# Expert outputs kept as rows in DRAM and fetched per token, in place of scatter products, in a two-layer hybrid decoder step

## The chip, the cores and the metric

The program runs on one core of one Trainium2 chip. The metric is the time of one execution on the device, in microseconds (us). The kernel before was timed three times: 1644.41, 1648.15 and 1650.19 us, median 1648.15 us. One further execution was profiled, and all durations below come from its trace.

## The reference

The program computes two layers of a decoder trunk for 320 tokens: a prompt of 256 and 8 samples of 8. Each layer has a mixer (window attention, a short convolution and memory attention, gated and summed) and a channel part, each followed by a layer norm. The channel part of layer 0 is one dense SwiGLU network; that of layer 1 is a mixture of 8 experts, of which each token uses two. The change is in and around the mixture:

```python
def _moe(x, w_router, b_router, wg, wu, wd):
    xt = x.reshape(-1, D_MODEL)                                  # 320 x 1024
    logits = jnp.dot(xt, w_router, ...) + b_router
    top_v, top_i = lax.top_k(logits, TOP_K)                      # 2 of 8
    top_w = jax.nn.softmax(top_v, axis=-1)
    gates = jnp.sum(one_hot(top_i, N_EXPERTS) * top_w[..., None], axis=1)
    y = jnp.zeros_like(xt)
    for e in range(N_EXPERTS):
        y = y + gates[:, e:e + 1] * _swiglu(xt, wg[e], wu[e], wd[e])   # D_FF = 2816
    return y.reshape(shp)

x <- LayerNorm(ALPHA * x + ffn(x))
```

## The kernel before, in words

All weights are float32 and pass through the core once. The stream is cut into units of 1 MiB (128 partitions x 2048 numbers). SyncE (SP) loads a unit into a slot of `raw`; ScalarE (ACT) copies it, rounded, to `high` (`hi_moe`, L775; L768 in the dense part); VectorE (DVE) subtracts the two and leaves the remainder in `low` (`lo_moe`, L1063; L1072); TensorE (PE) then makes three products per tile, high weight by high activation, low by high, high by low. The dense part has six slots of `raw`, the mixture eleven, and `high` has three everywhere. So SP may load unit n when PE has finished unit n-11 (n-6 in the dense part), and ACT may copy unit n when PE has finished unit n-3. Each engine runs its own list in the order in which it is written, and semaphores (`unit_done`, `hi_done`, `lo_done`) tie the lists together.

After the second mixer the router picks two experts per token. Every expert has 128 slots, and `one_hot` (DVE) marks which token goes to which slot. The experts are worked in pairs: `pair_of_experts` on every engine goes through 66 units, 33 for each of two experts (j = 0 and j = 1; n counts units of one expert). Four pairs are run here: the first, a loop body that runs `loops` times, and two more; more rounds would be run if an expert had over 128 tokens. At the end of a pair PE gathers the tokens of the next pair with one-hot products (`gather`, L1868 to L1870, after units 28 to 31 of j = 1). Each expert has a down projection into PSUM banks 0 and 1; when its last unit is done, ACT copies it, scaled by the gate of each slot, to `ygh` (L1017) and DVE leaves the remainder in `ygl` (L1464).

Around the change, in the kernel before:

- `slots_of` (L1876, PE, after units 6 and 7 of j = 0) transposes the one-hot marks into `slot`, which DVE copies out (L1448); `gates_of` (L1883, PE, after unit 8) takes the gate of each slot by small products. Both are done in every pair.
- `scatter` (L1891, L1892, PE) multiplies `slot` by `ygh` and `ygl`, which puts an expert's rows back to their tokens. The six groups of the pair before are done one after each of units 0 to 5 of the next pair, four products each, and DVE adds each to `acc` (`add_back`, L1429). The last pair's groups are done after its last unit.
- `gate_columns` (DVE, L1379 to L1383) splits the gates of the pair for `gates_of`; it ends DVE's part of the router, before the first `lo_moe` of the mixture.

POOL (GpSimd) makes masks, issues the DMAs of caches and small outputs in both mixers, and is idle after the router. The layer norm at the end works on `acc`.

Of the kernel before, what the change touches and what calls it, by code (L numbers as in the profile page):

```python
# [28 lines left out]
ALU = mybir.AluOpType  # L29
# [106 lines left out]
SCATTER_AFTER = {n: n for n in range(6)}  # L136
SLOTS_AFTER = {6: 0, 7: 1}
GATES_AFTER = 8
SCATTER_BANK = (7, 0, 1, 7, 0, 1)
# [83 lines left out]
def build_trunk(nc, A, O):  # L223
    with ExitStack() as ctx:
# [20 lines left out]
        def sem(name):  # L245
# [84 lines left out]
        place["at"] = scratch_at  # L330
        xtokh = take("xtokh", [P, 2, D], F32R)
# [6 lines left out]
        sil = take("sil", [P, 2, 512])  # L338
        ygh = take("ygh", [P, 2, D], F32R)
# [29 lines left out]
        place["at"] = moe_end  # L369
        xeh = at("xeh", [P, KD, 2 * P], F32R, x_at)  # L370
# [8 lines left out]
                         for s in range(RING, RING_MOE)]  # L379
        gain = at("gain", [P, D], F32, ring_at + 4 * UNIT)  # L380
# [83 lines left out]
        scat_mm = sem("scat_mm")  # L464
        scat_cp = sem("scat_cp")
# [11 lines left out]
        y_lo = sem("y_lo")  # L477
        fin_mm = sem("fin_mm")
# [89 lines left out]
        def _(sp):  # L568
# [54 lines left out]
            sp.wait_ge(dma_mid, 16 * (8 + 20 * 2))  # L623
            pair_of_experts(0, first=True)
# [20 lines left out]
        def _(pool):  # L645
# [57 lines left out]
            for l in range(2):  # L703
# [35 lines left out]
                pool.wait_ge(dma_mid, 16 * (8 + 20 * (l + 1)))  # L739

# [6 lines left out]
            pool.memset(ygl[:, :, :].bitcast(F32), 0.0).then_inc(y_lo, 1)  # L747
# [5 lines left out]
            pool.wait_ge(dma_out, 16 * 4)  # L753
        CONSTS = 7
# [4 lines left out]
        def _(act):  # L759
# [290 lines left out]
        def _(dve):  # L1050
# [326 lines left out]
            def gate_columns(step):  # L1377

                dve.tensor_copy(gcur[:, :, :], gates[:, :, bass.ds(step * 2, 2)]).then_inc(gcur_done, 1)  # L1379
                dve.wait_ge(gcur_done, step + 1)  # L1380
                dve.tensor_copy(gsplit[:, :, :, 0], gcur[:, :, :]).then_inc(gc_hi, 1)
                dve.wait_ge(gc_hi, step + 1)
# [33 lines left out]
            gate_columns(0)  # L1416
# [7 lines left out]

            def add_back(count, g):

                half = slice(512 * (g % 2), 512 * (g % 2) + 512)
                dve.wait_ge(scat_mm, count + (g + 1))
                dve.tensor_tensor(acc[:, g // 2, half], acc[:, g // 2, half], ps[:, SCATTER_BANK[g], :],  # L1429
                                  ALU.add).then_inc(scat_cp, 1)  # L1430

            dve.wait_ge(acc_cp, 6)
            def pair_of_experts(step, before=0, first=False, final=False):
                for m in range(NPAIR):
# [8 lines left out]
                    if j == 0 and not first and n - 1 in SCATTER_AFTER:  # L1443
                        add_back(before * 6, SCATTER_AFTER[n - 1])
                    if j == 0 and n - 1 in SLOTS_AFTER:
                        i = SLOTS_AFTER[n - 1]
                        dve.wait_ge(slot_mm, step * 3 + (i + 1))
                        dve.tensor_copy(slot[:, i, 0:T], ps[:, SLOT_BANK[i], 0:T]).then_inc(slot_cp, 1)  # L1448
                    if j == 0 and n - 1 == GATES_AFTER:
                        dve.wait_ge(slot_mm, step * 3 + 3)  # L1450
# [6 lines left out]
                    if j == 1 and not final and n == ONE_HOT_AT:  # L1457
                        one_hot(step + 1)
                        gate_columns(step + 1)
                    if j == 1 and not final and n - 1 in GATHER_AFTER:  # L1460
                        tokens_lo(step * 4 + 4, GATHER_AFTER[n - 1], GATHER_BANK[GATHER_AFTER[n - 1]])
                    if n == NX - 1:
                        dve.wait_ge(y_hi, step * 2 + (j + 1))
# [49 lines left out]
        def _(pe):  # L1513
# [387 lines left out]
            def pair_of_experts(step, before=0, first=False, final=False):  # L1901
                for m in range(NPAIR):
# [5 lines left out]
                    if unit[0] == "d":  # L1908
# [3 lines left out]
                        if i == 0:  # L1912
                            pe.wait_ge(y_lo, step * 2 + (j + 1))
# [25 lines left out]
                    if n in TURN_AFTER:  # L1939
# [3 lines left out]
                        if j == 0 and h == 1:  # L1943
                            pe.wait_ge(slot_cp, step * 3 + 2)
# [3 lines left out]
                    if j == 0 and not first and n in SCATTER_AFTER:  # L1948
# [80 lines left out]
```

## Time and profile before

| | |
|---|---|
| three runs | 1644.41, 1648.15, 1650.19 us; median 1648.15 us |
| the profiled execution | 1647.17 us |
| its span, first to last instruction | 1645.4 us |
| mean granted TensorE clock | 0.989 |
| PE busy in the span | 1594.8 us (97%) |
| DVE busy | 1123.1 us (68%) |
| ACT busy | 918.6 us (56%) |
| POOL busy | 62.1 us (4%) |
| DMA, mean over the span | 239 GB/s |

Busy times are of one execution and overlap each other. The end of a matmul is modelled, so matmuls of one row of work overlap in the table; the distance from one start to the next tells what a matmul costs. "Idle" of an engine stands with what ended it. The mixture begins at about 829 us of the span and its last product is at about 1632 us.

### The profile page before, as it was taken

How to read it: one execution, taken by the hardware profiler on the slowest of the kernel's cores; microseconds unless marked ns; L12 is line 12 of the kernel's file. 1: busy time of each engine (PE TensorE's matmuls, PEld its weight loads, DVE VectorE, ACT ScalarE, POOL GpSimd, SP SyncE). 2: the span in 40 equal slices, each digit the busy share in tenths (PEclk: the TensorE clock that was granted, in tenths of full speed). 3: DMA queues.
4: the chain of work that ended last, by engine and by line, in shares of the span. 5: the costliest groups of instructions: out<-in, count | busy, mean ns of one | idle time of the engine just before them, and what ended most of it. 6: DMA issues, size and time to landing. Idle time of an engine off the chain costs nothing.

```text
span 1645.4 us, 22946 instructions
## 1 busy us (share of the span) xinstructions
PE 1594.8 (97%) x9167; PEld 1407.3 (86%) x9167; DVE 1123.1 (68%) x1031; ACT 918.6 (56%) x938; POOL 62.1 (4%) x114
## 2 busy tenths in 40 slices
PE   7999999899999899999799999999999999999996
PEld 6999899799999789989588888888888888888885
DVE  5545546644434535566488898888888888888887
ACT  4544443433322544444477776677766777667775
POOL 4103000000000002000100000000000000000000
PEclk9999999999999999999999999999999999999999
DMA  9746344244444244342679999899998999989981
GB/s 300 251 132 197 103 128 141 91 154 152 146 142 150 77 141 148 127 108 98 231 252 363 369 366 319 299 368 365 367 322 296 369 367 362 319 306 366 365 325 58
DMA packets 213033, 392.51 MB, mean 239 GB/s; under 512 B 8000, under 2 KB 98512, under 8 KB 212896
## 3 DMA queue, kind: packets, MB, share of 16 engines
q1 hardware_dynamic: 207520, 376.99, 66.8%
q0 software_dynamic: 5408, 14.06, 2.7%
q8 instruction: 74, 1.21, 0.3%
q14 instruction: 31, 0.25, 0.1%
HBM read 388.22 MB, written 4.76 MB: 239 GB/s over the span
## 4 chain that ended last, share of the span: by engine, by line
PE 94%; DVE 3%; ACT 1%; DMA 1%; issue 1%; SPq 0%; ACTq 0%; DVEq 0%
PE ps L1516 12%; PE ps L1518 12%; PE ps L1517 12%; PE ps L1935 10%; PE ps L1937 10%; PE ps L1936 10%; PE ps L1919 5%; PE ps L1921 5%; PE ps L1920 5%; PE ps L1946 1%; PE ps L1665 1%; DMA raw<-in_w_mem_k_dram 1%; PE ps L1771 1%; PE ps L1765 1%; PE ps L1639 1%; PE ps L1891 1%
## 5 line engine op out<-in xcount | busy, mean ns | idle before, releaser
L1063 DVE TENSOR_TENSOR low<-raw,high 128x2048 fp32r<-128x2048 f32 x264 | 604.0, 2291 | 104.5 <-ACT high L775 103.9
L775 ACT ACTIVATE high<-raw 128x2048 fp32r<-128x2048 f32 x264 | 505.8, 1918 | 234.1 <-PE ps L1937 142.8
L1516 PE MATMUL ps<-xh,high 128*128 128x320 f32 x1088 | 343.3, 316 | 9.7 <-DVE xl L1247 9.4
L1072 DVE TENSOR_TENSOR low<-raw,high 128x2048 fp32r<-128x2048 f32 x90 | 205.8, 2291 | 214.4 <-ACT high L768 214.3
L1517 PE MATMUL ps<-xh,low 128*128 128x320 f32 x1088 | 338.9, 311 | 0.0
L1518 PE MATMUL ps<-xl,high 128*128 128x320 f32 x1088 | 338.6, 311 | 0.0
L1935 PE MATMUL ps<-high,xeh 128*128 128x512 f32 (+1 forms) x768 | 291.8, 380 | 1.0 <-ACT row_f L999 1.0
L1937 PE MATMUL ps<-high,xel 128*128 128x512 f32 (+1 forms) x768 | 288.1, 375 | 0.0
L1936 PE MATMUL ps<-low,xeh 128*128 128x512 f32 (+1 forms) x768 | 287.8, 375 | 0.0
L768 ACT ACTIVATE high<-raw 128x2048 fp32r<-128x2048 f32 x90 | 171.9, 1910 | 169.8 <-PE ps L1518 156.5
L1516 PEld LDWEIGHTS ps<-xh,high 128*128 128x128 f32 x1088 | 207.5, 191 | 19.4 <-issue 18.5
L1517 PEld LDWEIGHTS ps<-xh,low 128*128 128x128 f32 x1088 | 207.5, 191 | 0.0
L1518 PEld LDWEIGHTS ps<-xl,high 128*128 128x128 f32 x1088 | 207.2, 190 | 0.0
L1935 PEld LDWEIGHTS ps<-high,xeh 128*128 128x128 f32 x768 | 144.2, 188 | 29.7 <-DVE low L1063 1.3
L1937 PEld LDWEIGHTS ps<-high,xel 128*128 128x128 f32 x768 | 144.3, 188 | 28.8
L1936 PEld LDWEIGHTS ps<-low,xeh 128*128 128x128 f32 x768 | 144.3, 188 | 26.9
L1919 PE MATMUL ps<-high,heh 128*128 128x512 f32 x352 | 141.2, 401 | 0.0
L1921 PE MATMUL ps<-high,hel 128*128 128x512 f32 x352 | 139.2, 395 | 0.0
L1920 PE MATMUL ps<-low,heh 128*128 128x512 f32 x352 | 138.6, 394 | 0.0
L1921 PEld LDWEIGHTS ps<-high,hel 128*128 128x128 f32 x352 | 66.0, 188 | 16.3
L1920 PEld LDWEIGHTS ps<-low,heh 128*128 128x128 f32 x352 | 66.2, 188 | 14.6
L1919 PEld LDWEIGHTS ps<-high,heh 128*128 128x128 f32 x352 | 66.1, 188 | 14.5
(323 smaller groups left out, 1680.8 us busy)
## 6 DMA issues: line engine op xcount, KB each, us to landing
raw<-in_exp_w_gate_dram SPq DMA_DIRECT2D x88, 1024.0 KB, 5.3
raw<-in_exp_w_up_dram SPq DMA_DIRECT2D x88, 1024.0 KB, 5.4
raw<-in_exp_w_down_dram SPq DMA_DIRECT2D x88, 1024.0 KB, 5.3
raw<-in_w_in_dram SPq DMA_DIRECT2D x37, 1024.0 KB, 5.3
raw<-in_ffn_w_gate_dram SPq DMA_DIRECT2D x11, 1024.0 KB, 5.4
raw<-in_ffn_w_up_dram SPq DMA_DIRECT2D x11, 1024.0 KB, 5.3
raw<-in_ffn_w_down_dram SPq DMA_DIRECT2D x11, 1024.0 KB, 4.9
raw<-in_w_o_dram SPq DMA_DIRECT2D x8, 1024.0 KB, 5.2
```

Source lines behind the costliest of these rows:

```text
L775: act.activation(high[(N_DENSE + m) % HI_RING][:, :], raw_moe[s][:, :], ACT.Copy).then_inc(hi_done, 1)
L1063: dve.tensor_tensor(low_moe[s][:, :], raw_moe[s][:, :], high[(N_DENSE + m) % HI_RING][:, :].bitcast(F32), ALU.subtract).then_inc(lo_done, 1)
L1072: dve.tensor_tensor(low[n % RING][:, :], raw[n % RING][:, :], high[n % HI_RING][:, :].bitcast(F32), ALU.subtract).then_inc(lo_done, 1)
L1516: pe.matmul(out, wh, ah, start=first, stop=False)
L1517: pe.matmul(out, wl, ah, start=False, stop=False)
L1518: return pe.matmul(out, wh, al, start=False, stop=last)
L1919: pe.matmul(out, heh[:, tile, :], wh[:, c], start=i == 0 and k == 0, stop=False)
L1920: pe.matmul(out, heh[:, tile, :], wl[:, c], start=False, stop=False)
L1921: last = pe.matmul(out, hel[:, tile, :], wh[:, c], start=False, stop=i == NBLK - 1 and k == 1)
L1935: pe.matmul(out, xeh[:, k, slots], wh[:, c], start=k == 0, stop=False)
L1936: pe.matmul(out, xeh[:, k, slots], wl[:, c], start=False, stop=False)
L1937: last = pe.matmul(out, xel[:, k, slots], wh[:, c], start=False, stop=k == KD - 1)
```

## The change

Each finished expert's output is no longer put back by products, except for the last pair's. ACT copies it unscaled to `yraw` (two buffers that lie where `ygh` lies), SP stores it as 128 rows of 4 KB to a DRAM table `ybuf` with one row per expert slot, and DVE computes for each token, once in the router, the row numbers of its two experts (`place_idx`) and their gates (`share`). Choices that belong to the last pair get share 0 and row 0. In the last pair POOL fetches with six indirect loads, one per token tile and choice, 4 KB per token, and DVE adds each, times its share, to `acc`. Since rows that no expert wrote may be fetched, `ybuf` (24 x 128 rows, 12.6 MB) is filled with zeros in layer 0: POOL clears `zeros` after the last attention job there and issues twelve 1 MiB stores; ACT waits for them before the layer norm that ends layer 0. Scatter products, slot transposes, gate products and their DVE steps now stand in the last pair only.

```diff
-SCATTER_AFTER = {n: n for n in range(6)}
+ROW_AT = {26 + 4 * i: i for i in range(6)}
...
+        yraw = [nc.alloc_sbuf_tensor_at(f"yraw{j}", [P, D], F32, offset=ygh_at + 4 * D * j) for j in range(2)]
+        row_at = [rows_at + 4 * D * i for i in range(5)] + [rows_at]
+        ybuf = nc.dram_tensor("ybuf", (ROUNDS * NE * P, D), F32).ap()
+        zeros = at("zeros", [P, UNIT], F32, mem_kT_at)
...  SP
+                def store(j, rows_of):
+                    sp.dma_start(ybuf[rows_of, :], yraw[j][:, :]).then_inc(y_stored, 16)
                 for m in range(2, NPAIR if final else NPAIR + 2):
+                    if m == NX + RING_MOE + 2 and not final:
+                        sp.wait_ge(y_out, step * 2 + 2)
+                        store(0, slice(0, P) if first else bass.ds(before * 256 + 256, P))
+                    if m == RING_MOE + 2 and not first:
+                        sp.wait_ge(y_out, before * 2 + 3)
+                        store(1, bass.ds(before * 256 + P, P))
...  POOL, layer 0
+                if l == 0:
+                    pool.wait_ge(pv_mm, NJ)
+                    link(pool.memset(zeros[:, :], 0.0))
+                    for i in range(ROUNDS * NE // 2):
+                        pool.dma_start(ybuf[2 * P * i:2 * P * i + 2 * P, :].rearrange("(p r) n -> p (r n)", p=P),
+                                       zeros[:, :]).then_inc(y_blank, 16)
...  POOL, at its end
+            pool.wait_ge(y_stored, loops * 32 + 64)
+            pool.wait_ge(xe_lo, loops * 4 + 12)
+            pool.wait_ge(placed, 1)
+            for i in range(6):
+                t, tn = i // 2, TILES[i // 2][1]
+                if i == 5:
+                    pool.wait_ge(row_used, 1)
+                pool.indirect_dma_start(rows[i][0:tn, :], None, ybuf[:, :],
+                                        bass.IndirectOffsetOnAxis(ap=place_idx[0:tn, t, i % 2:i % 2 + 1], axis=0)
+                                        ).then_inc(row_ld[i], 16)
...  ACT
+            act.wait_ge(y_blank, 16 * ROUNDS * NE // 2)
             layer_norm(1, True, 32)
-                    if n == NX - 1:
+                    if n == NX - 1 and not final:
                         act.wait_ge(unit_done, step * NPAIR + (N_DENSE + m + 1))
-                        act.wait_ge(slot_cp, step * 3 + 3)
+                        if not first:
+                            act.wait_ge(y_stored, before * 32 + 16 * (j + 1))
+                        act.activation(yraw[j][:, :], ps[:, 0:2, :].rearrange("p b n -> p (b n)"), ACT.Copy).then_inc(y_out, 1)
...  DVE
-            gate_columns(0)
+            places()
+            def add_row(i):
+                t = i // 2
+                tn = TILES[t][1]
+                dve.wait_ge(row_ld[i], 16)
+                link(dve.scalar_tensor_tensor(acc[0:tn, t, :], rows[i][0:tn, :], share[0:tn, t, i % 2:i % 2 + 1], acc[0:tn, t, :],
+                                              ALU.mult, ALU.add))
-                    if j == 0 and not first and n - 1 in SCATTER_AFTER:
-                        add_back(before * 6, SCATTER_AFTER[n - 1])
+                    if j == 0 and final and n == 1:
+                        gate_columns(step)
+                    if final and m in ROW_AT:
+                        add_row(ROW_AT[m])
...  PE
                         if i == 0:
-                            pe.wait_ge(y_lo, step * 2 + (j + 1))
+                            if final and j == 1:
+                                pe.wait_ge(y_lo, 1)
+                            else:
+                                pe.wait_ge(y_out, step * 2 + (j + 1))
-                    if j == 0 and not first and n in SCATTER_AFTER:
-                        g = SCATTER_AFTER[n]
-                        scatter(ps[:, SCATTER_BANK[g], :], g, 0, True, False)
-                        scatter(ps[:, SCATTER_BANK[g], :], g, 1, False, True).then_inc(scat_mm, 1)
-                    if j == 0 and n in SLOTS_AFTER:
+                    if j == 0 and final and n in SLOTS_AFTER:
...
-                    if j == 0 and n == GATES_AFTER:
+                    if j == 0 and final and n == GATES_AFTER:
```

Three places show what moves. First PE, at the end of unit 0 of the loop body's pair (`high_62` is unit 0's weight, `high_63` unit 1's, `slot` and `ygh` the scatter). Before; the two products L1891 and L1892 stand there twice:

```order
L1937 MATMUL ps<-high_62,xel 128x512
L1951 ISA
L1952 REGISTER_ALU
L1891 MATMUL ps<-ygh,slot 128x512
L1892 MATMUL ps<-ygl,slot 128x512
L1906 REGISTER_ALU
L1929 REGISTER_ALU
L1935 MATMUL ps<-high_63,xeh 128x512
```

The same place now:

```order
L2014 MATMUL ps<-high_62,xel 128x512
L1980 REGISTER_ALU
L2006 REGISTER_ALU
L2012 MATMUL ps<-high_63,xeh 128x512
L2013 MATMUL ps<-low_180,xeh 128x512
```

The four scatter products between two units are gone; the same holds after units 1 to 5.

Second DVE, at the end of the router, up to the first `low` of the mixture (unit 2 of the first pair). Before:

```order
L1414 TENSOR_TENSOR gates<-oh_137,oh_138 128x3x8 x3
L1379 COPY gcur<-gates 128x6
L1381 CAST gsplit<-gcur 128x6
L1383 TENSOR_TENSOR gsplit<-gcur,gsplit 128x6
L1063 TENSOR_TENSOR low_172<-raw_165,high_61 128x2048
```

Now, where `places` stands (`top` and `chosen` are reused as its buffers). L1471 to L1475 stand there twice, once per choice, and L1478 and L1479 twice:

```order
L1464 TENSOR_TENSOR gates<-oh_137,oh_138 128x3x8 x3
L1471 COPY top<-topf 128x3
L1472 COPY top<-pair 128x3
L1473 TENSOR_TENSOR chosen<-iota_f,topf 128x24
L1474 SCALAR_TENSOR_TENSOR chosen<-posm,chosen 128x24
L1475 TENSOR_REDUCE top<-chosen 128x3
L1476 SCALAR_TENSOR_TENSOR top<-top 128x3x2
L1478 TENSOR_SCALAR chosen<-top 128x3x2
L1479 TENSOR_TENSOR top<-top,chosen 128x3x2
L1480 TENSOR_SCALAR cnt<-cnt 128x1
L1484 CAST topi<-top 128x3x2
L1113 TENSOR_TENSOR low_181<-raw_173,high_61 128x2048
```

Three short steps make room for twenty, ahead of the same subtraction (L1481 to L1483, three more of the twenty, are left out here).

Third DVE, in the last pair, where its second expert begins (`ygl` closes the first expert). Before:

```order
L1464 SCALAR_TENSOR_TENSOR ygl<-ps,gs,ygh 128x1024
L1062 REGISTER_ALU
L1063 TENSOR_TENSOR low_172<-raw_165,high_61 128x2048
L1063 TENSOR_TENSOR low_55<-raw_49,high_62 128x2048
L1063 TENSOR_TENSOR low_56<-raw_50,high_63 128x2048
```

Now:

```order
L1538 SCALAR_TENSOR_TENSOR ygl<-ps,gs,ygh 128x1024
L1112 REGISTER_ALU
L1113 TENSOR_TENSOR low_181<-raw_173,high_61 128x2048
L1113 TENSOR_TENSOR low_55<-raw_49,high_62 128x2048
L1493 SCALAR_TENSOR_TENSOR acc<-rows_160,top,acc 128x1024
L1113 TENSOR_TENSOR low_56<-raw_50,high_63 128x2048
```

The third of the six additions of fetched rows stands between two subtractions; the others stand four units apart, at units 26 and 30 of the first expert and 1, 5, 9 and 13 of the second.

## Rows read from the trace of the kernel before

**Rows 1.** The page, busy time of an engine: us, share, instructions.

```profile
PE 1594.8 (97%) x9167; PEld 1407.3 (86%) x9167; DVE 1123.1 (68%) x1031; ACT 918.6 (56%) x938; POOL 62.1 (4%) x114
```

**Rows 2.** Waits in the mixture: who for whom, us in total, times, longest.

```profile
ACT high L775 <- PE ps L1937: 141.6, 166, 1.8
DVE low L1063 <- ACT high L775: 99.7, 195, 1.5
PEld ps L1935 <- DVE low L1063: 1.1, 4, 0.3
```

**Rows 3.** Timeline of ACT, ends of the first three experts: start, us.

```profile
926.09 1.12 ACT L1017 ACTIVATE ygh<-ps,gs 128x1024 fp32r<-128x1024 f32 x1 [0.81 <-PE ps L1921]
...
1025.52 1.12 ACT L1017 ACTIVATE ygh<-ps,gs 128x1024 fp32r<-128x1024 f32 x1 [1.53 <-PE ps L1921]
...
1128.06 1.12 ACT L1017 ACTIVATE ygh<-ps,gs 128x1024 fp32r<-128x1024 f32 x1 [0.96 <-PE ps L1921]
```

**Rows 4.** Timeline of PE: units 0 and 2 begin, slots, gates.

```profile
828.99 0.47 PE L1935 MATMUL ps<-high,xeh 128*128 128x512 f32 x1 [0.98 <-ACT row_f L999]
...
834.62 0.40 PE L1935 MATMUL ps<-high,xeh 128*128 128x512 f32 x1
...
1050.92 0.58 PE L1876 MATMUL ps<-ident,onehot 128*128 128x128 f32 x3
...
1057.76 0.98 PE L1883 MATMUL ps<-gsplit,onehot 128*128 128x2 f32 x6
```

**Rows 5.** Timeline of DVE, end of the router.

```profile
830.63 0.16 DVE L1379 COPY gcur<-gates 128x6 f32<-128x6 f32 x1
...
831.03 0.17 DVE L1383 TENSOR_TENSOR gsplit<-gcur,gsplit 128x6 fp32r<-128x6 f32 x1
832.16 4.49 DVE L1063 TENSOR_TENSOR low<-raw,high 128x2048 fp32r<-128x2048 f32 x2 [0.96 <-ACT high L775]
```

**Rows 6.** DVE by line: count, duration ns least/median/most; page groups' mean ns.

```profile
L1429 DVE TENSOR_TENSOR acc<-acc,ps x18: 678/684/692, 1030.8 to 1452.3; 128x512 f32<-128x512 f32 x18
...
L1464 DVE SCALAR_TENSOR_TENSOR ygl<-ps,gs,ygh x8: 1276/1281/1286, 927.5 to 1627.9; 128x1024 fp32r<-128x1024 f32 x8
...
L1063 DVE TENSOR_TENSOR low<-raw,high 128x2048 fp32r<-128x2048 f32 x264 | 604.0, 2291 | 104.5 <-ACT high L775 103.9
```

**Rows 7.** Stretches of the mixture: us, busy of engines, clock, DMA share, GB/s.

```profile
840.00:1000.00 160.00, 160.00 (x736) 130.30 (x735) 139.97 (x85) 115.69 (x76) 0.00 (x0) 1.00 1.01 361
...
1030.00:1070.00 40.00, 40.00 (x180) 32.22 (x180) 33.31 (x26) 23.68 (x17) 0.00 (x0) 1.00 0.88 293
```

**Rows 8.** Loads of L608 on SP, issued 900 to 1000 us.

```profile
DMA to landing us min/median/max: 5.0/5.3/6.4
```

**Rows 9.** PE's last attention job of layer 0; loads on SP; POOL's issue, memset.

```profile
233.47 2.00 PE L1685 MATMUL ps<-pT,win_v 128*128 128x64 f32 x16
...
249.64 0.37 SPq L592 DMA_DIRECT2D raw<-in_ffn_w_gate_dram  x1
256.68 0.37 SPq L592 DMA_DIRECT2D raw<-in_ffn_w_up_dram  x1
...
145.96 0.94 POOL L674 DMA_DIRECT2D kstage<-in_cache_mem_k_dram  x1
...
L747 POOL MEMSET ygl<- x1: 1809/1809/1809, 795.6 to 795.6; 128x2048 f32 x1
```

**Rows 10.** DMA issues: KB each, median us to landing (at 55, 61, 1635).

```profile
out_win_v_sample_dram<-in_cache_win_v_dram POOLq DMA_DIRECT2D x2, 480.0 KB, 8.5
...
raw<-in_w_in_dram SPq DMA_DIRECT2D x1, 1024.0 KB, 11.5
...
out_y_prompt_dram<-yout SPq DMA_DIRECT2D x2, 512.0 KB, 2.6
```

**Rows 11.** Timeline at 125 us: a DVE subtraction beside eight POOL issues.

```profile
124.95 2.29 DVE L1072 TENSOR_TENSOR low<-raw,high 128x2048 fp32r<-128x2048 f32 x1 [1.07 <-ACT high L768]
124.99 4.03 POOL L729 DMA_DIRECT2D out_win_k_sample_dram<-kvtok  x8
```

More of the change, by code:

```diff
@@ L369, in build_trunk @@
         place["at"] = moe_end
+        yraw = [nc.alloc_sbuf_tensor_at(f"yraw{j}", [P, D], F32, offset=ygh_at + 4 * D * j) for j in range(2)]
+        place_tmp, place_row, share = top[:, :, 0:2], top[:, :, 2:4], top[:, :, 4:6]
+        place_idx, rank_e, limit = topi[:, :, 0:2], chosen, cnt[:, 0:1]
+        row_at = [rows_at + 4 * D * i for i in range(5)] + [rows_at]
+        rows = [nc.alloc_sbuf_tensor_at(f"rows{i}", [P, D], F32, offset=o) for i, o in enumerate(row_at)]
+        ybuf = nc.dram_tensor("ybuf", (ROUNDS * NE * P, D), F32).ap()
         xeh = at("xeh", [P, KD, 2 * P], F32R, x_at)
@@ L477, in build_trunk @@
         y_lo = sem("y_lo")
+        y_out = sem("y_out")
+        y_stored = sem("y_stored")
+        y_blank = sem("y_blank")
+        placed = sem("placed")
+        row_ld = [sem(f"row_ld{i}") for i in range(6)]
+        row_used = sem("row_used")
         fin_mm = sem("fin_mm")
@@ L746, in _ @@
             link(pool.memset(ygh[:, :, :].bitcast(F32), 0.0))
-            pool.memset(ygl[:, :, :].bitcast(F32), 0.0).then_inc(y_lo, 1)
+            pool.memset(ygl[:, :, :].bitcast(F32), 0.0).then_inc(y_out, 1)
             pool.affine_select(out=rank_of[:, :], in_=ones[:, :], compare_op=ALU.is_gt, fill=0.0,
@@ L1415, in _, with places @@
             link(last)
-            gate_columns(0)
+            def places():
+                e1 = [oh1, oh2]
+                for i in range(2):
+                    dve.tensor_copy(place_tmp[:, :, i:i + 1], topf[:, :, i:i + 1])
+                    dve.tensor_copy(share[:, :, i:i + 1], pair[:, :, 2 + i:3 + i])
+                    link(dve.tensor_tensor(rank_e[:, :, :], experts, wide(topf[:, :, i:i + 1]), ALU.is_equal))
+                    link(dve.scalar_tensor_tensor(rank_e[:, :, :], posm[:, :, :], 65536.0, rank_e[:, :, :], ALU.add, ALU.mult))
+                    link(dve.tensor_reduce(place_row[:, :, i], rank_e[:, :, :], AX, ALU.add))
+                link(dve.scalar_tensor_tensor(place_tmp[:, :, :], place_tmp[:, :, :], 128.0, place_row[:, :, :], ALU.mult, ALU.add))
+                for k in range(1, ROUNDS):
+                    link(dve.tensor_scalar(rank_e[:, :, 0:2], place_row[:, :, :], 128.0 * k, 128.0 * (NE - 1), ALU.is_ge, ALU.mult))
+                    link(dve.tensor_tensor(place_tmp[:, :, :], place_tmp[:, :, :], rank_e[:, :, 0:2], ALU.add))
+                link(dve.tensor_scalar(limit, cnt[:, 3:4], 256.0, 512.0, ALU.mult, ALU.add))
+                link(dve.tensor_scalar(place_row[:, :, :], place_tmp[:, :, :], limit, None, ALU.is_lt))
+                link(dve.tensor_tensor(share[:, :, :], share[:, :, :], place_row[:, :, :], ALU.mult))
+                link(dve.tensor_tensor(place_tmp[:, :, :], place_tmp[:, :, :], place_row[:, :, :], ALU.mult))
+                dve.tensor_copy(place_idx[:, :, :], place_tmp[:, :, :]).then_inc(placed, 1)
+            places()
[5 more added lines that the diff above has]
+                                              ALU.mult, ALU.add))
+                if i == 0:
+                    dve.tensor_copy(rank_e[:, 0, 0:1], share[:, 0, 0:1]).then_inc(row_used, 1)
             def hidden_lo(at, h):
@@ L1942, in pair_of_experts @@
                         pe.wait_ge(e_lo, at + (h + 1))
-                        if j == 0 and h == 1:
-                            pe.wait_ge(slot_cp, step * 3 + 2)
+                        if j == 0 and h == 1 and final:
+                            pe.wait_ge(slot_cp, 2)
                         for f in range(HIDDEN[h][1] // P):
```

55 lines of the change are left out of this document (24 added, 31 removed).

## The prediction

> **What bounds the kernel now.** I read the engines' busy times first, then the waits within the mixture, then timelines of single engines. PE is busy for 97% of the span [rows 1], which alone proves little, since the ends of matmuls are modelled. The waits settle it. In the mixture ACT waits for PE (142 us in 166 waits at one of its two causes), because a `high` slot comes free only when PE finishes a unit; DVE waits for ACT; PE waits for weights 1.1 us in all [rows 2]. No engine waits for a load. So PE sets the pace from 829 us on, and a product that leaves PE's list there moves the end by its whole cost, until something else becomes late. What that could be is the rest of the argument.
>
> PE's price per product: units 0 and 1 of the first pair are 24 products of 512 columns, and unit 2 begins 5.63 us after unit 0 [rows 4], so 0.235 us each (the 0.40 us that a row shows overlaps the next one). A unit of 12 such products is 2.8 us.
>
> **What goes.** Scatter: 6 groups x 4 products = 24 per pair, 24 x 0.235 = 5.6 us. A second way: the first pair has no scatter, and its first expert takes 926.09 - 828.99 = 97.1 us; the second pair's first expert takes 1128.06 - 1025.52 = 102.5 us [rows 3, 4]; the difference is 5.4 us, and the start of that interval lies some 0.2 us after PE began. The add-backs number 18 = 3 pairs x 6 [rows 6], so three pairs' scatters were among units, and all three go: 3 x 5.6 = 16.9 us. The last pair's own scatter stays. Slots and gates go from three pairs of four: two transposes of 0.58 us and one group of small products of 0.98 us per pair [rows 4], 2.1 us, in three pairs 6.4 us. Together 23.3 us of PE.
>
> DVE loses 18 additions of 0.68 us, three pairs' slot copies and six `ygl` of 1.28 us [rows 6]; none was waited for, so this is worth nothing by itself, but it keeps DVE behind PE: an expert without scatter needs 33 x 2.29 = 75.6 us of subtraction, twelve steps for its six hidden tiles at no more than 0.68 and one of 1.28, 85 us, against 33 units x 2.8 = 92 us of PE.
>
> **What comes, on the path.** (1) `places`. DVE ends the router at 830.63 and now has twenty short steps instead of three. Two steps of the same size start 0.40 us apart over two intervals, 0.20 us each [rows 5]; sixteen of the twenty wait for the one before, four do not and cost about 0.1: 3.6 us, to 834.2. The subtraction for unit 2 began at 832.16 (it waited for ACT) and ended 2.29 later at 834.4, just ahead of PE, which took unit 2 at 834.62 [rows 4, 5]. It now ends at 836.5, and PE stands for 2.0 us. Bounds: 1.3 us if the linked steps cost 0.16, 2.7 us if 0.24. After it DVE gains 0.5 us per unit on PE, so the wait does not come again.
>
> (2) The boundaries. When an expert ends, ACT's eviction holds back its next copy, and that is where PE's few waits for `low` stand (up to 0.3 us) [rows 2]. So far the scatter after unit 0 covered this at the starts of pairs. Three more such waits, 0.1 to 0.3 each: 0.5 us.
>
> (3) Adding fetched rows. Six additions of 128 x 1024 in the last pair; no row shows this form, the nearest is `ygl` at 1.28 us [rows 6]. Four units give DVE 4 x (2.8 - 2.29) = 2.0 us of room, but where an addition meets the multiplications and the remainders of the hidden tiles (0.68 each, as an add-back) there is none. Second expert, units 0 to 7: 8 x 2.29 + 3 x 0.68 + 2 x 1.28 = 22.9 us against 22.4. Stalls between 0 and 3 us; I take 1.5.
>
> **What comes, beside the path.** The six stores of 512 KB on SP's queue: a store of that size landed in 2.6 us [rows 10], and the wait ahead of it is for an eviction that ended two units before, so SP does not stand. Behind it are loads. A load is issued when unit n-11 ends, its copy is due when unit n-3 ends: 8 x 2.8 = 22.4 us, landing takes 5.3 and at most 6.4 [rows 8], so 16 us are spare and a store takes 1.4 of them (0.52 MB at 374 GB/s, the rate of 1.05 MB per 2.8 us). Cost nothing; the bound is the DMA rival below.
>
> The zero fill: the last attention job of layer 0 ends at 235.5, POOL clears 128 x 2048 (1.8 us, as for `ygl`) and issues twelve stores at 0.94 each [rows 9], so 12.6 MB enter the queues from about 237 to 249. Loads come each 7.04 us there [rows 9]; with six slots a load has 3 x 7.04 = 21.1 us until its copy is due, and PE needs the result two units later, 14.1 us, less 4.2 for copy and subtraction: 31 us in all. Low bound 0. High bound: the fill goes wholly ahead, at the only rate a store shows (512 KB in 2.6 us, 200 GB/s, [rows 10]): 63 us, and a load issued 3 us into it lands 60 us later, 29 too late. The nearest row is a 1 MiB load at 61 us beside four copies of 480 KB, whose landing grew from 5.3 to 11.5 us [rows 8, 10]: it was slowed, not shut out. I take 0.
>
> The Trainium skill, "DMA: Bandwidth & Descriptors", section "Queues, rings and completion order", has each DMA engine switch between queues after each packet. By that a load would get half the rate during the fill and land in some 10 us (an estimate), and the sum would be the same 0; strict order would give the high bound. The 11.5 us row lies on the side of sharing.
>
> The indirect loads: no row shows one. Low bound the 0.94 us of a plain issue [rows 9]; high bound one smallest issue per token, 4.03/8 = 0.50 us x 128 = 64 us per load [rows 11]. The last store goes out with unit 2 of the last pair, and rows are first wanted at unit 26: some 22 units, 62 us, of cover, then 11.2 us more for each. I take the low end, since 1 MiB of many short rows cost one issue of 0.94, not one for each; cost 0.
>
> POOL's issues may also hold DVE up, or DVE them. In the trace a subtraction beside eight issues of POOL took 2.29 us, its usual time, and the issues 0.50 each [rows 6, 11]; low bound 0, and high bound five issues of 0.94 in a row during which DVE stands, 4.7 us, of which 1.4 is slack. I take 0.
>
> The Trainium skill, "SBUF — State Buffer", section "Who interferes with whom", says that a DVE operation with two SBUF inputs and a POOL operation that reads SBUF shut each other out for a whole instruction. By that rule the high bound would come true if an indirect load counts as such a reader; the sum would be some 3 us worse. The rows of plain issues speak against it, and no row here has an indirect one.
>
> **Sum.** -23.3 + 2.0 + 0.5 + 1.5 = -19.3 us. The profiled execution took 1647.17, so 1627.9; it lay 0.98 under the median of the three runs, 1648.15, so 1628.9 us is the forecast. The three terms that it adds have bounds of 1.3 to 2.7, 0.3 to 0.9 and 0 to 3, and PE's part may be 0.7 larger by the bubbles around each group: 1626 to 1632.
>
> **The rivals.**
> DMA becomes the bound. For it: between 840 and 1000 us its busy share is 1.01 at 361 GB/s, and only where scatters stood does it fall to 0.88 [rows 7]. Those rests shrink. Against it: landing stays at 5.3 us, without growing, while PE takes 1.05 MB every 2.8 us [rows 8]. Price: a pair moves 69.2 + 1.05 MB, at 361 GB/s 194.6 us, and PE's new pair is 102.5 + 99.4 - 7.7 = 194.2 [rows 3], so the pairs are about even; the last one has 2.6 MB of rows on top, 7 us, and the stores may cost 1.4 each. Up to 10 us are given back: 1633 to 1640. Chance 0.09.
>
> The fill starves layer 0's loads, in part: 3 to 29 us are lost, likeliest some 8: 1637, at worst 1658. Chance 0.10, of which 0.06 still faster, 0.03 within 0.3%, 0.01 slower.
>
> POOL holds DVE up in the last pair, five issues in a row: DVE does no subtraction for 4.7 us and PE stands for 3.3: 1632. For it only that no indirect load was seen; against it the unchanged 2.29 us [rows 11]. Chance 0.04, still faster.
>
> Slower than before: the indirect loads come late. POOL works them one after another, DVE stands at `add_row` with all later subtractions behind it, and PE waits for `low`. The first is in time up to 62 us each; the fifth, wanted 62 + 45 us after the start, up to 21 us each: there it begins to cost. At 30 us each the fifth is 43 us late, a net loss of 24: 1672; at 64 us each well over 100. For it: nothing like it was measured. Against it: POOL is free then, and its plain issues cost under 1 us. Chance 0.07.
>
> The change does not do what it says, the products removed being hidden: the expert with scatter is 5.4 us longer than the one without [rows 3, 4], which excludes most of it. Chance 0.02, about 1648.
>
> **How the numbers follow.** Forecast 0.68. Outside it DMA 0.09, fill 0.10, POOL against DVE 0.04, late rows 0.07, no effect 0.02. Under 0.3%, 4.9 us, this kernel's runs can't tell a change from none. Faster: 0.68 + 0.09 + 0.06 + 0.04 = 0.87; same 0.03 + 0.02 = 0.05; slower 0.07 + 0.01 = 0.08. The range goes from 1622 (PE's part larger, no new wait) to 1640 (the DMA rival and the milder fill): left out are the late rows, the worse half of the fill and a few per cent below, some 0.17.
>
> **What would show it.** In the profile after: the interval between evictions of a pair's first expert down from 102.5 to about 95 us; PE waiting once, about 2 us, for `low` near 834 us, and not on loads; ACT still waiting for PE; landings of 1 MiB loads near 5 us, somewhat longer at 237 to 290 us and in the last pair; six additions of about 1.3 us, no wait ahead of them. Wrong would be: ACT waiting for DMA in the mixture or at 260 to 300 us, DVE waiting for row loads, or pairs that keep their 202 us.

## The result, and the profile after

The changed kernel took 1628.45 us (median of six runs, 1625.01 to 1635.63) beside 1646.58 for the kernel before (six runs, 1644.22 to 1652.43): ratio 0.989, 95% interval 0.9872 to 0.9909. In a second comparison it was 1628.71 beside 1650.25, ratio 0.987 (0.9848 to 0.9891). The forecast was 1628.9. The profiled execution took 1628.22 us, its span 1626.5.

The busy times of the page (us, share, instructions), to be held against [rows 1]:

```profile
PE 1574.2 (97%) x9059; PEld 1390.6 (86%) x9059; DVE 1109.9 (68%) x1016; ACT 918.7 (56%) x938; POOL 84.8 (5%) x135
```

PE has 108 instructions less and 20.6 us less of work, and is busy for 97% as before. The waits of the mixture (who for whom, us in total, times, longest) answer to [rows 2]:

```profile
ACT high L818 <- PE ps L2014: 127.0, 168, 2.4
DVE low L1113 <- ACT high L818: 97.0, 183, 2.2
...
PEld ps L2012 <- DVE low L1113: 4.2, 8, 2.2
...
PE ps L2012 <- DVE low L1113: 1.7, 1, 1.7
```

ACT still waits for PE, so PE still sets the pace; its waits for `low` grew from 1.1 us (1.3 from 829 us on) to 4.2, of which one takes 2.2. The evictions of the first three experts (ACT: start, us), as in [rows 3]:

```profile
927.79 1.03 ACT L1062 ACTIVATE yraw<-ps 128x1024 f32<-128x1024 f32 x1 [0.81 <-PE ps L1998]
...
1027.20 1.03 ACT L1062 ACTIVATE yraw<-ps 128x1024 f32<-128x1024 f32 x1 [1.53 <-PE ps L1998]
1122.02 1.03 ACT L1062 ACTIVATE yraw<-ps 128x1024 f32<-128x1024 f32 x1 [0.95 <-PE ps L1998]
```

The first expert of the second pair takes 1122.02 - 1027.20 = 94.8 us where it took 102.5. The longest wait is at unit 2 of the first pair, first on PE, then what DVE did ahead of it, as in [rows 4, 5]:

```profile
830.93 0.47 PE L2012 MATMUL ps<-high,xeh 128*128 128x512 f32 x1 [0.98 <-ACT row_f L1043]
...
838.44 0.50 PE L2012 MATMUL ps<-high,xeh 128*128 128x512 f32 x1 [1.73 <-DVE low L1113]
```

```profile
832.57 0.17 DVE L1471 COPY top<-topf 128x3 f32<-128x3 f32 x1
...
836.02 0.17 DVE L1484 CAST topi<-top 128x6 uint32<-128x6 f32 x1
836.10 4.49 DVE L1113 TENSOR_TENSOR low<-raw,high 128x2048 fp32r<-128x2048 f32 x2
```

The twenty steps last from 832.57 to 836.10, 3.5 us (3.6 expected), and unit 2 begins 7.5 us after unit 0 instead of 5.6. Stretches of the mixture (busy, clock, DMA share, GB/s), as in [rows 7]:

```profile
840.00:1000.00 160.00, 160.00 (x733) 130.52 (x732) 139.63 (x79) 116.34 (x77) 0.00 (x0) 1.00 1.01 365
1030.00:1070.00 40.00, 40.00 (x177) 32.21 (x176) 35.49 (x20) 29.40 (x20) 0.00 (x0) 1.00 1.03 379
```

Where scatters stood, DMA now moves 379 GB/s instead of 293: the rests are filled, as the DMA rival had it, but at a rate above the 361 that it took as the limit. Landings in the mixture (KB each, median us), as in [rows 8, 10], then the additions as in [rows 6]:

```profile
raw<-in_exp_w_up_dram SPq DMA_DIRECT2D x73, 1024.0 KB, 6.7
ybuf<-yraw SPq DMA_DIRECT2D x6, 512.0 KB, 7.4
...
rows<-ybuf,topi POOLq DMA_INDIRECT x6, 9.1
```

```profile
L1493 DVE SCALAR_TENSOR_TENSOR acc<-rows,top,acc x6: 1270/1278/1279, 1496.4 to 1554.2; 128x1024 f32<-128x1024 f32 x4, 64x1024 f32<-64x1024 f32 x2
its engine sat idle before it (us, times) until:
who waited for it (us, times):
```

The additions cost 1.28 us each and DVE never stood ahead of one. In layer 0 loads beside the fill landed late, and ACT waited for three of them (us, times):

```profile
DMA to landing us min/median/max: 10.4/16.7/27.1
```

```profile
  DMA raw<-in_w_o_dram: 9.9, 1
...
  DMA raw<-in_ffn_w_gate_dram: 5.0, 1
  DMA raw<-in_ffn_w_up_dram: 1.1, 1
```

**Lengths that all traces share.** Each profiled execution is cut at the same instructions: from the start of the last attention product of layer 0 (the last of the sixteen on PE in [rows 9]) to the start of DVE's reciprocal in the next layer norm, the one behind layer 0's mixer; from PE's first product of the first expert to the first eviction; from eviction to eviction; and from that first product to the end of the span. Second experts of pairs 1 to 3 took 99.4 to 99.5 us in every run and are left out.

| kernel | layer 0 stretch | first experts of pairs 1 / 2 / 3 / 4 | last expert | mixture to end |
|---|---|---|---|---|
| before | 60.17 | 97.10 / 102.54 / 102.57 / 102.52 | 94.65 | 816.4 |
| after | 60.80 | 96.87 / 94.82 / 94.73 / 97.01 | 95.06 | 795.5 |
| before, no scatter in pairs | 60.17 | 97.10 / 97.05 / 97.05 / 97.05 | 94.65 | 800.0 |
| before, no add-backs | 60.17 | 97.09 / 102.54 / 102.56 / 102.57 | 94.65 | 816.5 |
| after, no fill | 60.17 | 96.86 / 94.82 / 94.73 / 97.01 | 95.07 | 795.5 |
| after, row numbers spread | 60.85 | 94.86 / 94.82 / 94.73 / 97.01 | 95.05 | 793.5 |
| after, idle products | 60.84 | 96.85 / 100.25 / 100.17 / 102.45 | 95.07 | 811.8 |
| after, fill twice | 90.04 | 96.86 / 94.82 / 94.73 / 97.01 | 95.04 | 795.5 |
| after, rows wanted early | 60.81 | 96.86 / 94.82 / 94.72 / 106.53 | 94.79 | 804.8 |
| after, stores four times | 60.83 | 96.86 / 94.82 / 94.71 / 97.01 | 95.04 | 795.5 |
| no fill and spread | 60.17 | 94.88 / 94.82 / 94.71 / 97.01 | 95.05 | 793.5 |

A kernel that leaves a stretch alone repeats it within 0.1 us. The mixture's start does not repeat: without the second fill it lay between 823.5 and 833.0 us of the span, with no order by edit. That spread lies almost wholly in the two mixers, and it goes with the granted clock: from PE's first product to the last attention product of layer 0 the same executions took 225.6 us (clock 1.00) to 233.2 (0.96), through layer 1's mixer, from layer 0's closing norm to the norm behind that mixer, 255.4 (0.99) to 260.5 (0.97), and through layer 0's dense network between them 248.9 to 250.0. (1.00 is the level of 2.4 GHz; the other level, 1.2 GHz, would be 0.5.) This is why whole times of two executions differ by some us while the lengths in the table don't. Where expectations below speak of a spread of the dense layers, it is this one.

### The profile page after: what moved, and what is told of

It reads as the page before. It is cut to its first block, busy times and chain, and to the rows that moved or that the text cites. A ratio compares the mean times of both kernels' runs of the same rounds, so it can differ in the third digit from the quotient of the medians.

```text
span 1626.5 us, 22704 instructions
## 1 busy us (share of the span) xinstructions
PE 1574.2 (97%) x9059; PEld 1390.6 (86%) x9059; DVE 1109.9 (68%) x1016; ACT 918.7 (56%) x938; POOL 84.8 (5%) x135
## 4 chain that ended last, share of the span: by engine, by line
PE 92%; DVE 4%; DMA 3%; ACT 1%; issue 1%; SPq 0%; ACTq 0%; DVEq 0%
PE ps L1590 12%; PE ps L1591 12%; PE ps L1592 11%; PE ps L2012 10%; PE ps L2014 10%; PE ps L2013 10%; PE ps L1996 5%; PE ps L1998 5%; PE ps L1997 5%; DMA raw<-in_w_o_dram 2%; PE ps L2023 1%; DMA raw<-in_w_mem_k_dram 1%; PE ps L1739 1%; PE ps L1845 1%; PE ps L1839 1%; PE ps L1713 1%
## 5 line engine op out<-in xcount | busy, mean ns | idle before, releaser
L2014 PEld LDWEIGHTS ps<-high,xel 128*128 128x128 f32 x768 | 144.4, 188 | 29.1
```

Of the source, the lines that this page charges most:

```text
L2014: last = pe.matmul(out, xel[:, k, slots], wh[:, c], start=False, stop=k == KD - 1)
```

## The experiments

**1. Before, without the scatter of a pair in the next one** (PE's groups and DVE's additions are left out, so six experts' outputs are missing from the result).

```diff
-                    if j == 0 and not first and n in SCATTER_AFTER:
-                        ...
-                        scatter(ps[:, SCATTER_BANK[g], :], g, 0, True, False)
-                        scatter(ps[:, SCATTER_BANK[g], :], g, 1, False, True).then_inc(scat_mm, 1)
```

> The kernel before, without the scatter products that stand among units (3 x 24) and without the additions that take them up; slots and gates stay. The first three pairs are missing from its output. PE theory (a product on PE's list is worth its whole 0.235 us): 16.9 us under the kernel before, and the first expert of pairs two to four down from 102.5 to 96.9 us between evictions; PE then waits for low weights only at the boundaries, 0.3 us each. DMA rival (the stream of weights is about as slow as PE): well under 16.9 us, with ACT waiting for loads. DVE rival (what counts is the additions that DVE loses): also some 17 us here, so the next kernel tells those two apart.

Measured: 1632.53 us, ratio 0.991 (0.989 to 0.993). The evictions of the same three experts:

```profile
928.61 1.12 ACT L1017 ACTIVATE ygh<-ps,gs 128x1024 fp32r<-128x1024 f32 x1 [0.81 <-PE ps L1919]
...
1028.07 1.12 ACT L1017 ACTIVATE ygh<-ps,gs 128x1024 fp32r<-128x1024 f32 x1 [1.53 <-PE ps L1919]
1125.12 1.12 ACT L1017 ACTIVATE ygh<-ps,gs 128x1024 fp32r<-128x1024 f32 x1 [0.96 <-PE ps L1919]
```

1125.12 - 1028.07 = 97.05 against 102.54: 5.49 us per pair, 16.45 us from the mixture as a whole. This is the larger part of the gain, without a store or a fetch.

**2. Before, without the add-backs** (DVE's 18 additions are left out, and with them six experts' outputs; the products stay).

```diff
-                    if j == 0 and not first and n - 1 in SCATTER_AFTER:
-                        add_back(before * 6, SCATTER_AFTER[n - 1])
```

> The kernel before with all scatter products on PE, but without the 18 additions of 0.68 us on DVE that take them up (the first three pairs are missing from its output). PE theory: no change, within 2 us, and 102.5 us between evictions as before, since DVE is not waited for. DVE rival: up to 12 us less.

Measured: 1646.39 us, ratio 0.9995 (0.998 to 1.0009); no interval moved by more than 0.1 us. DVE's relief is worth nothing.

**3. After, with idle products in place of the scatter's.**

```diff
+                    if j == 0 and not first and n < 6:
+                        ...
+                        for _ in range(4):
+                            pe.matmul(ps[:, 7, :], heh[:, 12, :], ..., start=True, stop=True)
```

> The changed kernel, with 24 idle products of 512 columns put back on TensorE in each of the three pairs that lost their scatter, after units 0 to 5 of the pair's first expert, as many as the scatter had; they write into the free eighth bank of ps, which nothing reads. Storing, fetching and adding stay. Theory (the gain is TensorE time and nothing else): each of the three first experts of pairs 2 to 4 gets 24 x 0.235 = 5.6 us longer, 94.8 to 100.4 between evictions, the time rises by 16.9 us to about 1645, and the ratio to the kernel before is 0.998 to 1.001. Rival (part of the gain came from VectorE's or ScalarE's relief, which the products don't take back): under 12 us comes back, ratio under 0.996. Other rival (the products run in TensorE's idle time): under 3 us.

Measured: 1644.46 us, ratio 0.998 (0.9962 to 0.9999). On PE, one group of four and the product behind it:

```profile
1027.64 1.09 PE L2029 MATMUL ps<-hel,heh 128*128 128x512 f32 x4
1028.57 0.40 PE L2012 MATMUL ps<-high,xeh 128*128 128x512 f32 x1
```

Waits of PE for `low` in the mixture:

```profile
PEld ps L2012 <- DVE low L1113: 3.4, 5, 2.2
```

Four products take 0.93 us of PE's list, six groups 5.58, and the three intervals grew by 5.43 to 5.44: 16.3 us in all. The scatter's part of the gain is PE time, and what the stores and fetches cost does not show. An interval grew 0.15 us less than its products take. The likely reason is the boundary wait: the changed kernel has 8 such waits and this one 5, and the three that are gone, of 0.3 us each, stood at the starts of the three pairs.

**4. After, without the zero fill** (the fetches read from the six blocks that the stores write, which suffice for the routing of these inputs).

```diff
-                    link(pool.memset(zeros[:, :], 0.0))
-                    for i in range(ROUNDS * NE // 2):
-                        pool.dma_start(ybuf[...], zeros[:, :]).then_inc(y_blank, 16)
```

> The changed kernel without the zero fill of the DRAM table (no memset, no twelve stores, no wait for them); the indirect loads are given the 768 rows that three pairs write, all that these inputs use. My theory: the fill costs 0.3 us, the shift of the layer norm of layer 0 in the changed kernel's trace, although loads beside it took up to 27 us instead of 5, because a load has 31 us until PE needs it: 0 to 1 us less than the changed kernel, not to be told apart by the clock; the weight loads at 240 to 280 us land in 5.3 us again. Rival: the 1.9 us by which the mixture began later in the changed kernel are the fill's: 2 us less, and the mixture begins at 829.0.

Measured: 1624.27 us, ratio 0.9875 (0.9852 to 0.9898). The stretch of layer 0 goes back to 60.17 us and nothing else in the table moves: the fill costs 0.63 us, twice what the theory had, and the loads land in 5.3 to 5.4 us again. The rival is not borne out: the mixture began at 825.9 us here, but its start spreads by more than 2 us without any fill (823.5 to 833.0 in the two profiles of experiment 9). The times (1624.27 and 1628.45) can't show so little.

**5. After, with the fill twice.**

```diff
+                        pool.dma_start(yspare[...], zeros[:, :]).then_inc(y_blank, 16)
```

> The changed kernel, with the zero fill of 12 MB done twice, the second time into a second table that nothing reads, so 24 transfers of 1 MB on GpSimd's queue in layer 0. From layer 0's last attention product to its layer-norm reciprocal the kernels without a fill take 60.17 us and those with it 60.80 to 60.85; to the next reciprocal 248.86 and 249.6 to 249.8. Theory (fill and weight loads share the transfer engines, the loads land at 17 to 27 us instead of 5.3 and the weights in hand cover most of it): twice the fill lasts twice as long, no single load lands much later than 27 to 35 us, and the first stretch takes 61 to 65 us. Rival (the fill stands ahead of the loads in strict order): the load of w_o lands near 55 us, and the first stretch grows by 20 to 30 us. Other rival (the 0.65 us is the start of the fill alone, not its length): 60.8 again.

Measured: 1655.86 us, ratio 1.0043 (1.0025 to 1.0061), slower than the kernel before. Waits of ACT and PE between 230 and 560 us:

```profile
ACT high L814 <- DMA raw<-in_ffn_w_gate_dram: 18.5, 1, 18.5
ACT high L814 <- DMA raw<-in_ffn_w_up_dram: 16.5, 1, 16.5
...
PE ps L1593 <- DVE x L1282: 13.7, 2, 13.1
...
ACT high L814 <- DMA raw<-in_w_o_dram: 10.1, 1, 10.1
PE ps L1842 <- DVE x L1282: 9.6, 1, 9.6
```

ACT waited 45.1 us for loads, and behind it DVE, whose step `x` (the residual sum) stands in its list after a late subtraction, and PE, which stood for 23.3 us. The stretch grew from 60.17 to 90.04, by 29.9; the other 6.6 us fall where the granted clock was below full speed after these stops (0.52, 0.80, 0.71 and 0.61 in the four stretches of ten us from 280 to 320, between the levels of 1.2 and 2.4 GHz; 1.00 up to 280). With one fill ACT waited 16.0 us, PE stood for 0.4 and the stretch grew by 0.63. So the weight tiles ahead of PE cover most of the waits of one fill, and the 29.1 us that ACT waited more cost 29.2. The theory of this expectation, 61 to 65 us, is refuted: loads landed up to 52 us after issue. The rival's price came true (20 to 30 us), and its order nearly: the first load behind the start of the fill, w_o, issued when ten stores had been, was copied 27 us later, when ten had landed; the next overtook six stores (41 us), and the third landed right behind the last of them (52 us). One fill already reaches the edge of the cover, since PE stood for 0.4 us; how much more would be free was not run.

**6. After, with the row numbers computed between weight tiles** (in four pieces after units of the first expert).

```diff
+PLACES_AT = {12: 0, 18: 1, 24: 2, 44: 3}
-            places()
+                    if first and m in PLACES_AT:
+                        places(PLACES_AT[m])
```

> The changed kernel with the twenty steps of places cut into four parts of about 1 us, each put behind a subtraction within the first pair (units 12, 18, 24 of the first expert and 11 of the second) instead of at the end of the router. My theory: PE's one wait of about 2 us before unit 2 of the first pair goes, and no new one comes since DVE has some 1.4 us of room there: 1.9 us less, first expert 95.0 us from first product to eviction instead of 96.9. Rival (the router's end is not on the path, or each part costs PE as much where it now stands): no change.

Measured: 1624.9 us, ratio 0.9871 (0.9849 to 0.9893). PE's first product and ACT's first eviction are 94.86 us apart instead of 96.87, so the stall is worth 2.0 us:

```profile
831.64 0.47 PE L2017 MATMUL ps<-high,xeh 128*128 128x512 f32 x1 [1.01 <-ACT row_f L1044]
```

```profile
926.50 1.03 ACT L1063 ACTIVATE yraw<-ps 128x1024 f32<-128x1024 f32 x1 [0.81 <-PE ps L2003]
```

**7. After, with the fetched rows wanted early.**

```diff
-ROW_AT = {26 + 4 * i: i for i in range(6)}
+ROW_AT = {4 + 4 * i: i for i in range(6)}
```

> The changed kernel, with the six additions of fetched rows moved from units 26, 30, ... 46 of the last pair to units 4, 8, ... 24, so that the first stands on VectorE at about 1434 us of the span, while its indirect load is issued at 1432.5 and landed after 9 us. Theory (VectorE runs its list in order, and what waits behind the row is the next low-order weight tile): VectorE stands 7 to 10 us once, at the first row; it was about 1.6 us ahead of TensorE at the places, so TensorE loses 5 to 9 us in the first expert of the last pair, 97.0 becoming 102 to 106, and the time rises by that much; the five later rows have landed and cost nothing. Rival (the ring of weight tiles covers it): under 1 us. Other rival (every row is late, six waits of 8 to 10 us): over 25 us.

Measured: 1636.97 us, ratio 0.9931 (0.9907 to 0.9955). The waits from 1420 to 1530 us, and PE in the ten us in which its wait ends, at 1441.6 (busy, clock, DMA share, GB/s):

```profile
DVE acc L1493 <- DMA rows<-ybuf,topi: 8.6, 1, 8.6
...
PE ps L2012 <- DVE low L1113: 7.3, 1, 7.3
```

```profile
1440.00:1450.00 10.00, 8.42 (x28) 0.69 0.86 269
```

DVE stood once, for the first row, and handed 7.3 of its 8.6 us on to PE. The interval grew by 9.5 us, to 106.5, a little above the 102 to 106 of the theory, which had no term for the clock: after the wait it was 0.69 over these ten us (0.97 in the ten before, 1.00 in the ten behind, between the levels of 1.2 and 2.4 GHz). PE did 28 products in 8.4 us there and 48 in the next ten; at that pace 28 take 5.8 us, so the clock cost about 2.6, of the size of the other 2.2. The mechanism of the "late rows" rival exists, and 22 units of distance are what keeps it away.

**8. After, with every store four times** (9.4 MB more).

```diff
-                    sp.dma_start(ybuf[rows_of, :], yraw[j][:, :]).then_inc(y_stored, 16)
+                    for table in (ybuf, *ycopies):
+                        sp.dma_start(table[rows_of, :], yraw[j][:, :]).then_inc(y_stored, 16)
```

> The changed kernel, with each of the six stores of 128 x 1024 rows issued four times, the three extra into tables that nothing reads: 9.4 MB more in all over three pairs, in bursts of 2 MB after each eviction. The evictions two experts later wait for all four. Theory (TensorE sets the pace, the ring of weight tiles covers a burst): the intervals between evictions stay at 94.8 and 99.4 within 0.5 us, 0 to 3 us in all, with weight loads beside a burst landing at 10 us instead of 6. Rival (the transfer engines are full and set the pace, every byte more costs its time): 9.4 MB at 345 GB/s is 27 us, about 4.5 us per expert.

Measured: 1627.4 us, ratio 0.9865 (0.9839 to 0.9891); the mixture takes 795.5 us again. Issues from 920 to 1630 us (KB each, median us to landing):

```profile
raw<-in_exp_w_up_dram SPq DMA_DIRECT2D x74, 1024.0 KB, 10.3
...
ycopy<-yraw SPq DMA_DIRECT2D x18, 512.0 KB, 9.0
ybuf<-yraw SPq DMA_DIRECT2D x6, 512.0 KB, 7.1
```

Weight loads land in about 10 us (medians 9.9 to 10.3) instead of 6 (5.9 to 6.7), and nobody waits for one. A busy share of 1.00 of the DMA engines in this stream is not a bound: from 920 to 1520 us they moved 378 GB/s at a share of 1.02, against 365 at 1.01 without the copies, and four times the change's stores cost nothing.

**9. Both improvements together, twice, and the changed kernel again beside the second.** The edits are those of 4 and 6.

> The changed kernel with two edits together: no zero fill (the fetches read from the first six blocks of 128 rows alone, all of which the stores have written with this routing; without the fill the loads of layer 0 land in 5.3 us again), and the row numbers computed in four pieces between the first expert's weight tiles instead of ahead of the first. Theory (the two costs are in different stages and add): the first expert takes 94.9 us instead of 96.9, from layer 0's last attention product to its layer-norm reciprocal 60.2 instead of 60.8, and 2 to 4 us less in all than the changed kernel, a ratio of 0.986 to 0.9875 to the kernel before, near 1625 beside a before of 1648. Rival (the two gains are one, or the spread of the dense layers hides them): the ratio stays at 0.989.

> The changed kernel, unaltered, beside the version without fill and with spread row numbers on the same chip. Its profile gave 60.80 us in the stretch with the fill, 96.87 us for the first expert and 795.6 us from the mixture's first expert product to the end. Theory: the same lengths again, and 2.6 us more than the other version, of which 2.0 in the first expert and 0.6 in the stretch with the fill; what the times differ by beyond that is the spread of the dense layers. Rival (a cost that these stretches don't show, since the medians of the two were 1628.5 and 1622.3 in different calls): 5 to 8 us more again.

> The version without fill and with spread row numbers, once more, beside the changed kernel. Theory: first expert 94.9 us, stretch of layer 0 60.2 us, 793.5 us from the first expert product to the end, and 2.6 us under the changed kernel by these stretches. Rival: 5 to 8 us under it, as the medians of two separate calls had it.

Measured: 1622.3 us, ratio 0.9837 (0.9814 to 0.986), in the first comparison. In the second it took 1626.82 beside 1628.71 for the changed kernel, ratios 0.9861 (0.9838 to 0.9883) and 0.987 (0.9848 to 0.9891). The lengths are as the theory has them, 60.17, 94.88 and 793.5 against 60.81, 96.86 and 795.5: 2.6 us. The 6 us between medians of separate comparisons did not return; the rival is dropped. Its layer 0 stretch and its mixture are as short as any in the table, but the times of the second comparison alone do not set it apart from the change.

## Why the prediction was right

**PE sets the pace: shown.** Taking PE's products away gave 5.49 us per pair (experiment 1), putting as many back took 5.44 (3), and relieving DVE alone gave nothing (2).

**Scatter, 16.9 us, and boundary waits, 0.5: both right.** The idle products of experiment 3 take 5.58 us per pair, 16.7 in three. What the interval loses is 5.49 or 5.44, about 0.1 to 0.15 us less, since a wait that the scatter had covered appears; three of them are 0.3 to 0.45 us.

**Slots and gates, 6.4 us: 6.8.** First experts fall from 97.05 without scatter to 94.82 and 94.73 after, 2.2 and 2.3 us; in the first pair, with the row numbers out of the way, from 97.10 to 94.86, 2.2. The prediction named bubbles around the groups as a reason for up to 0.7 more.

**The row numbers, 2.0 us: 2.0**, by experiment 6, and by the place that the prediction gave: the 3.5 us of steps, less the 0.57 of the three that they replace and the 0.96 that DVE had waited for ACT [rows 5].

**Adding fetched rows, 1.5 us: 0.4.** The last expert went from 94.65 to 95.06, the one before it from 97.05 to 97.01. The duration was right (1.28); what was too large was the stall. The working counted 22.9 us of DVE against 22.4 of PE and gave DVE no lead for the 0.5; what the trace has near the additions is one new wait of PE for `low`, of 0.41 us at 1523.75.

**The fill, 0: 0.63, and that is partly luck.** One of the prediction's own signs of being wrong did appear: ACT waited for loads at 260 to 300 us, 16 us in all, and PE lost next to nothing by it only because of the cover. Loads landed at up to 27.1 us, near the 31 us that the prediction worked out as that cover. The prediction took 0 because its nearest row spoke for sharing, a load of 11.5 us beside four copies; that was too small a burst to size twelve. The stores' issues and landings (the longest is the last store's):

```profile
L766 POOL DMA_DIRECT2D ybuf<-zeros x12: 534/534/569, 237.4 to 243.2; - x12
...
DMA to landing us min/median/max: 4.3/9.3/30.9
```

The last store landed at 274.1, and the load issued at 249.3 behind all twelve only at 276.5: the fill went nearly wholly ahead, as in the high bound. What was wrong in that bound was the rate, and this kept the loss small: 12.6 MB in 36.7 us are 343 GB/s, where it had taken 200 GB/s and 63 us. The Trainium skill, "DMA: Bandwidth & Descriptors", section "Queues, rings and completion order", has the DMA engines switch between queues after each packet. The prediction's estimate from it, half the rate and a landing in 10 us, was too low here: 27.1 us.

**Stores, 0: 0**, though the 2.6 us from a quiet queue became 7.4 in the stream; there was cover for that. **Indirect loads, 0: 0.** They took 0.95 to 2.91 us to issue, one to three times the low bound of 0.94 and far from the 64 of the high one, and 8 to 10 to land; experiment 7 shows the price if they come late.

**Sum.** In the lengths: 816.4 to 795.5 is -20.9, and +0.6 in layer 0: -20.3, against -19.3 forecast. The 1.0 us between them is rows (-1.1), slots and gates (-0.4) and fill (+0.6), with 0.1 left. The two comparisons gave -18.1 and -21.5; the 3.4 us between them are within the spread of the mixers. That the forecast met the first median within 0.5 us is partly luck.

**The rivals.** DMA as a bound: refuted by experiment 8; its 361 GB/s was the rate that PE asked for, not what the engines could give. The fill: real, but it took a second fill to reach the price. No effect: refuted by 1 and 3. Late rows: the first load was issued at 1432.5 us and landed in 8 to 10, and its row was wanted at 1496.4, so the rival was some 54 us from biting. POOL holding DVE: the other way round, below.

## What to carry to other kernels

A DMA busy share of 1.00 did not say here how much was left: the share was 1.01 at 361 GB/s and 1.02 at 417 to 419 beside the fill (250 to 270 us). Add traffic and see whether anyone waits before calling it a bound. Cover is a stock, here nearly all of the 16 us that ACT waited for loads beside one fill, and a cost of nothing inside it says nothing of the next transfer; the same burst twice cost 47 times as much (29.9 against 0.63 us). And compare traces by lengths between the same instructions: they repeat within 0.1 us where whole times spread by several, and they price edits of 0.4 to 2 us that no timing here could tell from no change.

## What the hardware showed that was not expected

An indirect load's issue on POOL waits for a running subtraction of DVE. The issues on POOL, then the subtractions on DVE over the same time, in the changed kernel:

```profile
1432.51 2.24 POOL L794 DMA_INDIRECT rows<-ybuf,topi  x1 [1.06 <-issue]
1435.05 2.44 POOL L794 DMA_INDIRECT rows<-ybuf,topi  x1 [0.30 <-issue]
...
1441.01 0.95 POOL L794 DMA_INDIRECT rows<-ybuf,topi  x1 [0.30 <-issue]
```

```profile
1431.55 2.29 DVE L1113 TENSOR_TENSOR low<-raw,high 128x2048 fp32r<-128x2048 f32 x1 [0.51 <-ACT high L818]
1434.35 2.29 DVE L1113 TENSOR_TENSOR low<-raw,high 128x2048 fp32r<-128x2048 f32 x1 [0.50 <-ACT high L818]
...
1441.01 2.33 DVE L1113 TENSOR_TENSOR low<-raw,high 128x2048 fp32r<-128x2048 f32 x1
```

The first two begin while a subtraction runs and end 0.91 and 0.85 us after it (five of the six do so, by 0.78 to 0.91); the one that begins with the subtraction takes 0.95 us and DVE's instruction 0.04 us more than usual. In experiment 7, where DVE stood, five issues in a row took 0.92 to 1.02 us:

```profile
1432.04 0.97 POOL L794 DMA_INDIRECT rows<-ybuf,topi  x1 [0.30 <-issue]
1433.32 0.95 POOL L794 DMA_INDIRECT rows<-ybuf,topi  x1 [0.30 <-issue]
```

The prediction had asked whether POOL would hold DVE up; it was POOL that waited, up to 2 us an issue, and nobody waited for POOL. The Trainium skill, "SBUF — State Buffer", section "Who interferes with whom", has the two shut each other out, with the one that issues first going through. The rows agree for POOL's side; for DVE's they don't show it, since the subtraction beside the 0.95 us issue took 0.04 us more and no more.
